# Two transformer blocks on one core: gate by weighted sums on VectorE, key norm tile by tile, bias rows spread later

## What is computed

```python
mod = silu(c) @ w_ada + b_ada                    # one row of 3072
shift, scale, gate = split(mod, 3)
h = rms_norm(x, norm_g) * (1 + scale) + shift
ssm_u, ssm_z, q, k, v, attn_z, q_idx, k_idx, w_idx = split(h @ w_in)
y_ssm  = s5_mixer(ssm_u, ...) * silu(ssm_z)      # state space, gelu, then a gated linear unit (w_glu)
# attention: scores of an indexer pick the 128 best keys of each query (top-k, by threshold);
# q and k are normed per head; logits get a bias by distance from rel_bias; softmax; values
y_attn = dsa_mixer(q, k, v, q_idx, k_idx, w_idx, q_gain, k_gain, rel_bias) * silu(attn_z)
x = x + gate * (concat(y_ssm, y_attn) @ w_out)
x = second_block(x)                              # pooling and sparse attention, then an ffn
```

## Time and profile before

| | us |
|---|---|
| median of 3 runs | 1405.61 (1402.22 to 1407.60) |
| the profiled execution, its own time | 1405.56 |
| its span, first to last instruction | 1403.7 |
| busy in the span: TensorE | 1369.1 |
| VectorE | 797.1 |
| ScalarE | 351.0 |
| GpSimd | 268.1 |

### The profile page before, as it was taken

The page is one execution under the profiler, slowest core; times in us unless marked ns, Lnnn a source line. Parts: engine busy times, 40 slices in busy tenths (PEclk is TensorE's granted clock), DMA queues, the critical chain, the costliest instruction groups (busy, mean ns, idle before and its releaser), DMA issues.

```text
span 1403.7 us, 16136 instructions
## 1 busy us (share of the span) xinstructions
PE 1369.1 (98%) x5852; PEld 855.4 (61%) x5852; DVE 797.1 (57%) x1916; ACT 351.0 (25%) x859; POOL 268.1 (19%) x265
## 2 busy tenths in 40 slices
PE   4999999999999999999999999999999999999998
PEld 2444555545544545655555666444578888888887
DVE  6778769638541463113555666112557677777474
ACT  4213121115300102111455666010022323220000
POOL 1168487205102286600000000000000000000000
PEclk9999999899999999999999999999999999999999
DMA  9592324342403112301201001120323131314120
GB/s 343 166 191 75 102 54 141 94 158 90 150 1 109 60 60 66 115 30 50 101 1 61 1 2 61 32 89 0 105 76 104 61 120 60 120 61 165 60 68 30
DMA packets 85657, 120.58 MB, mean 86 GB/s; under 512 B 15208, under 2 KB 43182, under 8 KB 85580
## 3 DMA queue, kind: packets, MB, share of 16 engines
q1 hardware_dynamic: 80880, 110.80, 25.3%
q10 hardware_dynamic: 2956, 5.05, 1.1%
q0 software_dynamic: 1744, 3.70, 0.9%
HBM read 111.00 MB, written 6.84 MB: 84 GB/s over the span
## 4 chain that ended last, share of the span: by engine, by line
PE 86%; DVE 6%; DMA 3%; POOL 2%; issue 1%; SPq 1%; ACT 1%; DVEq 0%; ACTq 0%; POOLq 0%
PE bank L802 20%; PE bank L1370 17%; PE bank L1396 9%; PE bank L1274 6%; PE bank L815 5%; PE bank L837 5%; PE bank L1084 4%; PE bank L1229 3%; PE bank L1254 3%; PE bank L868 2%; PE bank L1340 2%; PE bank L1129 2%; DVE arena L2307 1%; DVE arena L2306 1%; PE bank L1071 1%
## 5 line engine op out<-in xcount | busy, mean ns | idle before, releaser
L802 PE MATMUL bank<-arena 128*128 128x512 f32 (+1 forms) x800 | 341.2, 583 | 0.0
L802 PEld LDWEIGHTS bank<-arena 128*128 128x128 f32 x800 | 150.0, 191 | 169.3 <-issue 164.8
L1370 PE MATMUL bank<-arena 128*128 128x256 f32 x1120 | 242.0, 379 | 0.0
L1370 PEld LDWEIGHTS bank<-arena 128*128 128x128 f32 x1120 | 212.7, 190 | 29.7 <-issue 0.8
L1396 PE MATMUL bank<-arena 128*128 128x256 f32 x616 | 133.1, 379 | 0.0
L837 PEld LDWEIGHTS bank<-arena 128*128 128x128 f32 (+2 forms) x692 | 82.4, 143 | 74.2 <-issue 47.0
L1396 PEld LDWEIGHTS bank<-arena 128*128 128x128 f32 x616 | 117.0, 190 | 15.9
L815 PE MATMUL bank<-arena 128*128 128x512 f32 x256 | 116.5, 609 | 0.0
L837 PE MATMUL bank<-arena 128*128 128x128 f32 (+2 forms) x692 | 96.1, 277 | 18.4 <-ACT arena L1484 6.8
L1877 POOL TENSOR_TENSOR arena<-arena 128x1 f32<-128x1 f32 x8 | 4.4, 555 | 466.5 <-DVE arena L2088 466.5
L2616 DVE CUSTOM_DVE_ANT_0 arena<-bank,arena 128x128 f32<-128x128 f32 (+3 forms) x128 | 57.9, 489 | 58.5 <-PE bank L1229 57.5
(11 more groups left out here) (346 smaller groups left out, 1737.8 us busy)
## 6 DMA issues: line engine op xcount, KB each, us to landing
arena<-in_w_in SPq DMA_DIRECT2D x14, 2048.0 KB, 7.8
arena<-in_w_up SPq DMA_DIRECT2D x20, 1024.0 KB, 6.8
arena<-in_w_ada SPq DMA_DIRECT2D x8, 1024.0 KB, 13.7
arena<-in_w_down SPq DMA_DIRECT2D x8, 1024.0 KB, 7.3
arena<-in_w_ada SPq DMA_DIRECT2D x2, 2048.0 KB, 8.6
arena<-in_w_out SPq DMA_DIRECT2D x2, 2048.0 KB, 8.4
arena<-in_w_attn_br SPq DMA_DIRECT2D x2, 2048.0 KB, 8.0
arena<-in_w_o SPq DMA_DIRECT2D x2, 2048.0 KB, 7.8
```

The costliest lines, as they stand in the source:

```text
L802: mm = pe.matmul(ps[:, 0:n], act[:, k, 128 * t:128 * t + 128], w[:, k, 0:n], start=(k == 0), stop=(k == kt - 1))
L1370: mm = pe.matmul(ps, left[:, k, :], right[:, k, :], start=(first and k == 0), stop=(k == 3), skip_group_check=True)
```

## The change

- The gate is formed as the modulation columns are: VectorE adds the eight weighted rows of each half (`gate_sums`, 16 instructions) between the z and az parts, and TensorE spreads each sum over all rows by one product with a 128 by 128 block of ones (`onesb`). `silb` and its copy go. Chunk gate 1 becomes two loads of 1 MB into free places, issued with the write-back of y 3; the glu and all later chunks change slots. The fill work is 18 products instead of 32, dealt out by `FILL1_TO`. GpSimd's load of x for the residual waits for the sums.
- The key norm is made tile by tile inside top-k of row 1, roots on VectorE; GpSimd's root goes. Top-k of row 1 is cut 4, 1, 11, all of row 2 and 7 rounds of row 3 come before scan 2. The query norm comes behind the gelu inputs of y 0 and 1, still ahead of scan 3.
- The bias row products stand between and behind modulation turns 0 and 1, their copies around ScalarE's first two parts of h; the spread in DRAM is issued behind `ssm_out(0)`.
- In both pair loops the out parts after the last scores come ahead of the turn.

```diff
+        gm = [score[:, 0, :], kiT]
+        gate1 = [arena[:, XROW0:XROW0 + 2048].rearrange("p (a b) -> p a b", a=4), qiT]
+        onesb = arena[:, SSM0 + 14656:SSM0 + 14784]
...
-        FILL1_MM = [(key, k) for key in FILL1_TILES for k in range(4 if key[0] == "glu" else KT)]
+        FILL1_MM = [(key, k) for key in FILL1_TILES for k in range(4 if key[0] == "glu" else 1)]
+        FILL1_TO = [1, 2, 2, 2, 4, 6, 8, 10, 12, 13, 14, 16, 17, 18, 18, 18]
...
+        chunk(("gate", 0), ("gsum", 1), KT, 512, [(0, 512, lambda: cols_of(w_ada, 0, KT, 2048, 2560))])
...
-                if name == ("gate", 0):
-                    ssm_back(3)
...
+                if name == ("gate", 0):
+                    aux_ready(sp_, ("qt", 3))
+                    sp_.dma_start(gate1[1], cols_of(w_ada, 4, KT, 2560, 3072)).then_inc(gate1_in[1], 16)
+                    ssm_back(3)
+                    sp_.dma_start(gate1[0], cols_of(w_ada, 0, 4, 2560, 3072)).then_inc(gate1_in[0], 16)
...
+            x_turns("x", xrow, (xn_done, TT))
+            pe.wait_ge(pool_ones, 1)
+            mod_turn(0)
             pe.wait_ge(rb_in_s, 16)
             pe.wait_ge(rb_one, 1)
             pe.wait_ge(onehot_in, 16)
-            for name, c0, n in (("rb", 0, 512), ("rb2", 512, 128)):
...
+            rb_rows("rb2", 512, 128)
             mod_turn(1)
+            rb_rows("rb", 0, 512)
...
+                    if kind == "gate":
+                        kt = 1
+                        pe.wait_ge(gsum_done, j + 1)
+                        mm = pe.matmul(fbank(key)[:, :], onesb, gm[j], start=True, stop=True)
...
-                if 0 <= n - 2 < NS1:
-                    pair_turn(n - 2)
                 if n == NS1:
                     pe.wait_ge(lg_done, 2 * NS1)
                     aux_out(pe, ("pv", 3))
                     out_part(0, 0, (4, 5))
                 if n == NS1 + 1:
                     out_part(0, 0, (6, 7))
+                if 0 <= n - 2 < NS1:
+                    pair_turn(n - 2)
...
+            rb_in_rows("rb2", 512, 128)
             h_even(0)
             h_even(2)
+            rb_in_rows("rb", 0, 512)
...
-            act.wait_ge(rb_saved, 16)
-            act.dma_start(rb_dram, rb_one_dram.unsqueeze(1).broadcast_to((8, 128, 640))).then_inc(rb_spread, 16)
...
             ssm_out(0)
+            act.wait_ge(rb_saved, 16)
+            act.dma_start(rb_dram, rb_one_dram.unsqueeze(1).broadcast_to((8, 128, 640))).then_inc(rb_spread, 16)
             rels(3)
...
-                if q == 2:
-                    pool.wait_ge(ksq_done, 1)
-                    step(pool.tensor_scalar(stat[:, 16:48], stat[:, 16:48], 1.0 / 64, EPS, ALU.mult, ALU.add))
-                    pool.tensor_tensor(stat[:, 16:48], stat[:, 16:48], halves, ALU.pow).then_inc(kroot_done, 1)
...
+            pool.wait_ge(gsum_done, 2)
             pool.dma_start(xrow[:, 0:2, :], x_rows[:, 0:2, :]).then_inc(x_again[0], 16)
...
+            def gate_sums(j, ks):
+
+                for k in ks:
+                    if j == 0:
+                        w = weights(v, ("gate", 0))[:, k, :]
+                    else:
+                        v.wait_ge(gate1_in[k // 4], 16)
+                        w = gate1[k // 4][:, k % 4, :]
+                    if k == 4 * j:
+                        ins = v.tensor_scalar(gm[j], w, silc[:, k:k + 1], None, ALU.mult)
+                    else:
+                        ins = v.scalar_tensor_tensor(gm[j], w, silc[:, k:k + 1], gm[j], ALU.mult, ALU.add)
...
-            topk(1, 14)
+            head_squares("k", row, (0, 1))
+            topk(1, 4)
+            head_squares("k", row, (2,))
+            root(slice(16, 40), 1.0 / 64)
+            head_scales(None, knorm_done, row, (0, 1, 2))
+            topk(1, 1)
             scan(1)
-            topk(1, TOPK // 8 - 14, True)
-            head_norm("k", None, knorm_done, row, on_pool=True)
-            topk(2, 8)
+            head_norm("k", None, knorm_done, row, (3,))
+            topk(1, TOPK // 8 - 5, True)
+            topk(2, TOPK // 8, True)
+            topk(3, 7)
             scan(2)
-            topk(2, TOPK // 8 - 8, True)
-            topk(3, TOPK // 8, True)
-            head_norm("q", None, qnorm_done, qiT)
+            topk(3, TOPK // 8 - 7, True)
             gelu_in(0)
             gelu_in(1)
+            head_norm("q", None, qnorm_done, qiT)
             scan(3)
...
             z_in(3)
+            gate_sums(0, range(KT))
             az_in(0)
+            gate_sums(1, (4, 5, 6, 7))
             gelu_in(3)
             az_in(1)
+            gate_sums(1, (0, 1, 2, 3))
             gelu_out(3)
...
-            v.wait_ge(aux_done, AUX[("y", 3)] + 1)
-            v.tensor_copy(silb, silc[:, 0:8].unsqueeze(2).broadcast_to((128, KT, 128))).then_inc(silb_done, 1)
```

More of the change, by code:

```diff
@@ L278, in program, with fill1_mm @@
         name_fill(*FILL1_TILES)
-        FILL1_MM = [(key, k) for key in FILL1_TILES for k in range(4 if key[0] == "glu" else KT)]
-        assert len(FILL1_MM) == 2 * NS1
+        FILL1_MM = [(key, k) for key in FILL1_TILES for k in range(4 if key[0] == "glu" else 1)]
+        FILL1_TO = [1, 2, 2, 2, 4, 6, 8, 10, 12, 13, 14, 16, 17, 18, 18, 18]
+        assert len(FILL1_TO) == NS1 and FILL1_TO[-1] == len(FILL1_MM)
+        def fill1_mm(n):
+            return range(FILL1_TO[n - 1] if n else 0, FILL1_TO[n])
         def fill1_ends(n):
-            return [FILL1_MM[m][0] for m in (2 * n, 2 * n + 1)
+            return [FILL1_MM[m][0] for m in fill1_mm(n)
                     if m + 1 == len(FILL1_MM) or FILL1_MM[m + 1][0] != FILL1_MM[m][0]]
@@ L406, in program @@
             w1chunk(name, (name, 3), c0)
-        for j in range(2):
-            chunk(("gate", j), ("fill", ("gate", j)), KT, 512,
-                  [(0, 512, lambda j=j: cols_of(w_ada, 0, KT, 2048 + 512 * j, 2560 + 512 * j))])
+        chunk(("gate", 0), ("gsum", 1), KT, 512, [(0, 512, lambda: cols_of(w_ada, 0, KT, 2048, 2560))])
         chunk("glu", ("fill", ("glu", 3)), 4, 512, [(0, 512, lambda: cols_of(w_glu, 0, 4, 0, 512))])
@@ L538, in program @@
         topk_done = sem("topk_done")
-        ksq_done = sem("ksq_done")
-        kroot_done = sem("kroot_done")
+        gsum_done = sem("gsum_done")
+        gate1_in = [sem(f"gate1{a}_in") for a in range(2)]
         knorm_done = sem("knorm_done")
@@ L547, in program @@
         pn1_done = sem("pn1_done")
-        silb_done = sem("silb_done")
         gbias_done = sem("gbias_done")
@@ L743, in _ @@
                         sp_.wait_ge(dpair_done, res)
+                    elif kind == "gsum":
+                        sp_.wait_ge(gsum_done, res)
                     elif kind == "product":
@@ L1056, in pair_fill @@
             def pair_fill(n):
-                for key, k in FILL1_MM[2 * n:2 * n + 2]:
+                for m in fill1_mm(n):
+                    key, k = FILL1_MM[m]
                     kind, j = key
-                    if k == 0:
-                        if kind == "gate":
-                            pe.wait_ge(silb_done, 1)
-                        else:
-                            pe.wait_ge(z_done, TT)
-                        weights(pe, key if kind == "gate" else "glu")
-                        if FUSE[key]:
-                            pe.wait_ge(bank_free[FBANK[key]], FUSE[key])
-                    s_, _, kt, cols = CH[key if kind == "gate" else "glu"]
-                    w = slot_view(s_, kt, cols)
-                    if kind == "gate":
-                        mm = pe.matmul(fbank(key)[:, :], silb[:, k, :], w[:, k, :], start=(k == 0), stop=(k == kt - 1))
-                    else:
+                    if k == 0 and FUSE[key]:
+                        pe.wait_ge(bank_free[FBANK[key]], FUSE[key])
+                    if kind == "gate":
[3 more added lines that the diff above has]
+                    else:
+                        w = weights(pe, "glu")
+                        kt = w.shape[1]
+                        if k == 0:
+                            pe.wait_ge(z_done, TT)
                         mm = pe.matmul(fbank(key)[:, :], w[:, k, 128 * j:128 * j + 128], zz[:, k, :],
@@ L1477, in _ @@
                 act.activation(sqx, xrow[:, t, :], ACT.Square, accum_out=stat[:, t:t + 1]).then_inc(sq_done, 1)
-                if t == 1:
-                    for name, c0, n in (("rb", 0, 512), ("rb2", 512, 128)):
-                        aux_ready(act, name)
-                        act.activation(rb_row[0:8, c0:c0 + n], abank(name)[0:8, 0:n], ACT.Copy).then_inc(afree(name), 1)
             for t in range(TT):
```

55 lines of the change are left out of this document (31 added, 24 removed).

## The result

The changed kernel takes 1392.38 us (median of 4, 1390.94 to 1393.19) where the kernel before took 1406.61 beside it: ratio 0.990, interval 0.987 to 0.993. Run again among the experiments it took 1393.64 (0.992, 0.990 to 0.994). So 12 to 14 us came of the 20.5 forecast (14.2 here, 12.0 in the repeat).

The account below looks back on a forecast made before the run. The prediction took TensorE, busy 98% of the span, as the bound, its stalls being the other lever. Terms 5.1 + 0.7 + 7.8 + 6.3 + 0.6 = 20.5 us off 1405.56 gave 1385, range 1377 to 1396.

Parts of the forecast that it names:

- the u write: Rival at the write of u to DRAM: its own pattern, not the bias spread, makes it 11 us; 1390, chance 0.15.
- half the output wait: From the rival that the last state output still waits, query norm and gelus stretched by GpSimd's work: 1393, chance 0.10.
- mask, norms and 5 rounds to 155, where scan 1 meets its input: Key norm step: VectorE, from the scores' end at about 140, reaches scan 1 at 155, when its input is ready.
- TensorE has four banks of lead: Bias spread step: TensorE's lead over VectorE's index scores and first scan, if these come late; 0.5 us taken off.
- U, 5.1: State-space inputs: moving the bias spread speeds the u write, removing a 2.2 us stall and halving 6.8 at half clock.
- Key norm, 0.7: Third z table: 1.7 us gained without GpSimd's root, less 1.0 charged for scan 2 standing later on VectorE.
- Query norm, 7.8: Last state output: query norm behind the gelu inputs shortens last z part to second az column; gain 7.8 us.
- Gate and pairs, 6.3: First block's pairs: fewer gate products gain 3.5 us, out parts ahead of the turn 2.1, the dropped copy 0.7.
- Second block's reorder, 0.6: End of the second block's pairs: out parts ahead of the turn remove a TensorE stall of 0.6 us.
- Start, 0: Bias row products and copies moved at the start: taken as 0, ends -1.5 and +1.0 us.
- The clock falls in the pairs: Rival in the pairs: TensorE, thinly busy without the gate's products, drops to half clock; +4 us, 1389, chance 0.15.
- Slower: scan 2: Rival at state output 2: scan 2 delays TensorE, slower overall from 20 us late on, 22 late is 1408; chance 0.03.

Follow-up runs that it names:

- a5: Changed kernel with the turns of both blocks put ahead of the out parts again, as before the change: 1393.01 us (0.991).
- a9: Changed kernel with the query norm put back ahead of the two gelu inputs, nothing else: 1393.30 us (0.992).
- c1: Changed kernel with the gate part alone undone, 16 products of 512 columns in the pairs again: 1398.83 us (0.997).
- a7: Changed kernel with scan 1 ahead of the key norm's scales, tile 3's norm in GpSimd's gap, scan 2 behind 2 rounds of row 3: 1386.57 us (0.987).
- a3: Changed kernel with the bias spread issued again ahead of the u copies, all else kept: 1394.71 us (0.993).
- b4: Kernel before with the key norm part alone, including the new places of scans 1 and 2: 1401.97 us (0.998).
- b3: Kernel before with the gate part alone (weighted sums, two products, weights and their issues): 1404.21 us (0.998).
- a1: Changed kernel with scan 1 moved ahead of the key norm's root and three scales, behind three more top-k rounds: 1410.05 us (1.003).
- a2: Changed kernel with scan 1 ahead of the key norm's root and scales, and scans 2 and 3 made early too: 1404.83 us (1.000).
- a10: a7 with 12 rounds of row 2 instead of 13, and the 512 bias row product ahead of modulation column 1: 1387.03 us (0.987).
- b1: Kernel before with the bias spread alone moved behind the first state output: 1400.48 us (0.997).

## Why the prediction was right in the range and wrong in its likeliest case

The time lies in the range (1377 to 1396), 7.4 us above the forecast of 1385. The range was there for other reasons, so that the time lies in it says little for the working; and its upper end is not what the two terms named for it give (1385 + 5 for the u write + 4 for half the output wait is 1394). By its own test the forecast failed: az had to end by 294 and ended at 298.9. No rival named the cause either; the two that gave 1390 and 1393 put the loss elsewhere and are both refuted (a write of 4.4 us, no wait at output 3).

**The step that failed** is in the key norm: "mask, norms and 5 rounds to 155, where scan 1 meets its input". The input was there at 156.2; VectorE was at 160.4. I had priced squares, root and scales at their quiet lengths although scales of 8.69 us for four were among my own rows, and I used those only against the rival about scan 2. Ahead of scan 1 the root took 4.3 us, two of its instructions 1.14 and 1.17 instead of 0.18, each ending with the GpSimd product that had begun just before it (at 156.2 and 154.8). The mask took 1.90 us where it had taken 0.94, the third squares 1.72 instead of 0.69: with the root's 2.0 that is 3.9 us of stretching. Without it scan 1 would have stood at about 156.4, with its input. (That it was not 155 comes mostly of the scores, which ended at 142.0 and not at 140.) And with U earlier TensorE came 4.4 us sooner, so scan 1 should have come that much sooner too: "TensorE has four banks of lead" held for the scores, not for the state chain. The price was 3.5 us of wait and 5.0 of lower clock in the changed kernel's two traces; behind the same wait a5, a9 and c1 lost 3.3. Run a7 gives 7.1 of the 8.5 back with the same work in another order.

Point by point:

- **U, 5.1:** right as a part (5.3 alone, write 4.4 us, clock 1.00 behind U). In the changed kernel TensorE has all of its 4.4 us at output 1 and waits 3.5 there; what the move alone is worth there, a3 doesn't say.
- **Key norm, 0.7:** right by chance (0.8 alone, within the spread of the runs): more loss at outputs 1 and 2 than charged, and a gain at output 3 that I had put elsewhere. Scan 2, in my sum at 204.3, was at 212.4.
- **Query norm, 7.8:** the size was right (8.2), the cause was not. The order is worth nothing (a9); the wait went with the key norm part (b4), most likely because VectorE no longer stands still 10 us for GpSimd's root.
- **Gate and pairs, 6.3:** 7.5 measured. First logits to pair 14 normed took 50.6 us (300.21 to 350.85), not 53.0: VectorE sets the pace, at 95% busy (47.28 of 49.60), but needed 2.3 us of waits for which I had 3.5, and its busy time grew by 0.6 us (48.3 from 47.7) where I had 1.8 for glu tile 3, now inside. The sums waited 8.1 us for their weights and ended at 293.8, not at 284, still 5 us before az. The out parts' 2.1 were not there; the gate part carries all of it.
- **Second block's reorder, 0.6:** the wait went, as shown by its return in a5. From the rest of out to the end it takes 1.0 us longer all the same, by one more dip of the clock (at 595 and at 625, before at 635).
- **Start, 0:** not contradicted, within 1.5 us by which traces of any of these kernels differ.
- **"The clock falls in the pairs" (0.15, +4 us):** not in the two traces of the changed kernel, nor in a7 and b3. But in six other traces with the weighted sums (a1, a2, a3, a5, a9, a10) it fell once or twice there, 1.6 to 1.7 us each, and in none of the four with the 16 products (before, b1, b4, c1). So the rival was real, at 1.6 to 3.3 us, and comes and goes; ten traces against four are not many.
- **"Slower: scan 2":** 22 us late was to be 1408. In a1 scan 2 is at 226.1, 22 us after the forecast's 204, and the time is 1410.05.

On the stretching, the Trainium skill, SBUF — State Buffer, section "Who interferes with whom", says that a VectorE operation with both inputs in SBUF contends with GpSimd's reads, that whoever issues first has the shared port pair for its whole instruction, and that on trn2 tensor_reduce never contends. These traces agree: the squares go from 0.69 to 3.10 us, the reduce behind them stays at 0.69, and top-k rounds of row 1 keep their 0.98. Two inputs are not needed for it here: in a1 L2088 and L2089, tensor_scalar with one input, took 1.15 and 1.94 us instead of 0.17. With that rule I would have put two-input work into GpSimd's gaps to begin with; it was the rule that spoke against this change, and the prediction didn't weigh it.

## What to carry to other kernels

When a part moves TensorE earlier, ask of each engine that feeds the next stage whether it can move too: what was on time by the old clock is late by the new one, and the gain is waited out there. Price an instruction by the row with the same neighbour beside it, not by its quiet length, and put VectorE work that stretches (products of two tensors and tensor_scalar here) where GpSimd is idle, top-k rounds and reductions where it is busy; the order alone was worth 7 us of span here and cost 16.5 the other way. A part's worth on its own and its worth beside the others can differ by nearly all of it (the gate 0.4 us of span alone, 5.0 with the others), so measure both; and look in both traces where the difference comes from, since one of 0.8 us can be a sum of several larger ones (a3).

## What the runs showed of the hardware beyond that

- A stall and the clock: behind waits of 1.69 (a3), 1.67 (b4), 1.10 (b1) and 0.22 us (a7) at output 1 the granted clock stayed at 1.00 (2.4 GHz); behind 3.48 us there it fell to 0.50 (1.2 GHz), and 5.0 us were lost in the changed kernel's two traces, 3.3 in a5, a9 and c1. But behind waits of 1.49 and 1.53 us at output 2 (b4, a3) it fell as well, costing 3.4 us, as did 2.25 us at U (before). Neither does the length of the wait alone decide whether the clock falls, nor does it fix what that costs.
- The clock falls where TensorE is busy all the time too: in the second block, at 585 to 655 us, every trace but one (a5) has one or two stretches of 5 us or so near 0.67, 1.6 to 1.7 us lost in each, and b3 loses 6.9 us. These, the ones in the pairs and the start move a single trace by 1 to 5 us.
